# Second DeltaNet half prepared inside the first half's last level

## What is computed

```python
def layer(h, l):
    u = rms_norm(h, attn_norm_w[l])
    (dn_q, dn_k, dn_v, dn_z, dn_b, dn_a, df_q, df_k, df_v, ml_cq, ml_ckv, ml_kr) = split_columns(u @ w_in[l])
    y_dn = gated_deltanet(...)     # two directions, chunked, 4 heads of 128
    y_df = diff_attention(...)     # 4 heads, p0 - lam * p1
    y_ml = mla_attention(...)      # 4 heads, 128 + 64 rotary
    h = h + concatenate([y_dn, y_df, y_ml]) @ w_out[l]
    u = rms_norm(h, ffn_norm_w[l])
    return h + (swiglu(u) if l % 2 == 0 else moe_swiglu(u))   # layer 1: top 2 of 8 experts

def chunk_gated_delta_rule(q, k, v, beta, g):      # per chunk, gc = cumsum(g)
    decay = exp(gc[i] - gc[j]) for i >= j
    a_mat = strict_lower((beta * k) @ k.T * decay)
    value = solve(I + a_mat, beta * v)
    k_cumdecay = solve(I + a_mat, beta * k * exp(gc))
    v_new = value - k_cumdecay @ state
    out = (q * exp(gc)) @ state + ((q @ k.T) * decay) @ v_new
    state = state * exp(g_last) + (k * exp(g_last - gc)).T @ v_new
```

## Time and profile before

| what | us |
|---|---|
| three runs | 1918.44, 1910.54, 1918.0 (median 1918.0) |
| profiled execution, its own time | 1916.52 |
| span of that execution | 1914.7 |
| TensorE busy | 1859.5 (97%) |
| VectorE busy | 1468.5 (77%) |
| ScalarE busy | 1121.1 (59%) |
| GpSimd busy | 101.3 (5%) |
| mixers of layer 0 | from about 136 to 300 |
| mixers of layer 1 | from about 689 to 850 |

### The profile page before, as it was taken

One profiled execution on the slowest core, in us unless ns is written; L12 is line 12 of the kernel. 1 busy time (PEld: TensorE's weight loads), 2 busy tenths in 40 slices (PEclk: granted clock), 3 DMA queues, 4 the chain that ended last, 5 costly groups with the idle time before them and its releaser, 6 DMA issues.

```text
span 1914.7 us, 26250 instructions
## 1 busy us (share of the span) xinstructions
PE 1859.5 (97%) x10606; PEld 1577.0 (82%) x10606; DVE 1468.5 (77%) x1732; ACT 1121.1 (59%) x1241; POOL 101.3 (5%) x95
## 2 busy tenths in 40 slices
PE   9997989999999989989999999999999999999998
PEld 8985768999999967679788888888888888888886
DVE  8759667555459657766888889889888888898986
ACT  5644424433345635344777777777776777777775
POOL 0014030000000022110000000000000000000000
PEclk9999989999999989999999999999999999999999
DMA  7400014454444000034899999999998999999994
GB/s 302 155 29 1 1 34 166 163 172 170 157 177 154 24 28 1 16 118 176 330 353 360 350 350 354 346 350 356 348 362 340 349 351 353 366 352 363 355 363 174
DMA packets 64192, 443.51 MB, mean 232 GB/s; under 512 B 8172, under 2 KB 8204, under 8 KB 13632
## 3 DMA queue, kind: packets, MB, share of 16 engines
q1 hardware_dynamic: 62032, 437.87, 61.6%
q0 software_dynamic: 1760, 3.78, 0.6%
q10 hardware_dynamic: 272, 0.10, 0.0%
HBM read 440.66 MB, written 2.17 MB: 231 GB/s over the span
## 4 chain that ended last, share of the span: by engine, by line
PE 88%; DVE 10%; issue 1%; ACT 1%; DMA 0%; SPq 0%; DVEq 0%; ACTq 0%
PE ps L1951 23%; PE ps L1953 23%; PE ps L1952 23%; PE ps L1964 2%; DVE w_lo L1229 2%; DVE cacc L1321 2%; PE ps L2384 1%; PE ps L2568 1%; PE ps L2370 1%; PE ps L2189 1%; PE ps L2579 1%; PE ps L2389 1%; PE ps L2236 1%; PE ps L2274 1%; PE ps L2273 1%
## 5 line engine op out<-in xcount | busy, mean ns | idle before, releaser
L1286 DVE TENSOR_TENSOR m_lo<-raw,m_hi 128x2048 fp32r<-128x2048 f32 x336 | 768.3, 2289 | 135.9 <-ACT m_hi L864 135.7
L864 ACT ACTIVATE m_hi<-raw 128x2048 fp32r<-128x2048 f32 x336 | 644.1, 1918 | 269.1 <-PE ps L1953 269.1
L1951 PE MATMUL ps<-m_hi,xe_hi 128*128 128x512 f32 x896 | 358.6, 400 | 0.0
L1952 PE MATMUL ps<-m_hi,xe_lo 128*128 128x512 f32 x896 | 353.6, 395 | 0.0
L1953 PE MATMUL ps<-m_lo,xe_hi 128*128 128x512 f32 x896 | 353.6, 395 | 0.0
L1229 DVE TENSOR_TENSOR w_lo<-raw,w_hi 128x1024 fp32r<-128x1024 f32 (+1 forms) x164 | 183.2, 1155 | 105.6 <-ACT w_hi L829 105.6
L1951 PE MATMUL ps<-u_hi,w_hi 128*128 128x272 f32 x800 | 235.1, 294 | 6.5 <-DVE w_lo L1229 4.4
L1953 PE MATMUL ps<-u_lo,w_hi 128*128 128x272 f32 x800 | 231.5, 289 | 0.0
L1952 PE MATMUL ps<-u_hi,w_lo 128*128 128x272 f32 x800 | 230.4, 288 | 0.0
L829 ACT ACTIVATE w_hi<-raw 128x1024 fp32r<-128x1024 f32 (+1 forms) x164 | 159.5, 1002 | 115.0 <-PE ps L1953 106.0
L1953 PEld LDWEIGHTS ps<-m_lo,xe_hi 128*128 128x128 f32 x896 | 168.0, 187 | 41.1
(11 more groups left out here) (404 smaller groups left out, 2610.7 us busy)
## 6 DMA issues: line engine op xcount, KB each, us to landing
raw<-in_moe_units SPq DMA_DIRECT2D x336, 1024.0 KB, 4.9
raw<-in_dense_units SPq DMA_DIRECT2D x57, 1024.0 KB, 5.0
raw<-in_dense_units SPq DMA_DIRECT2D x16, 768.0 KB, 5.6
raw<-in_dense_units SPq DMA_DIRECT2D x8, 896.0 KB, 4.5
w_uq<-in_mla_w_uq SPq DMA_DIRECT2D x2, 768.0 KB, 4.4
mats<-in_c_mats POOLq DMA_DIRECT2D x1, 1216.0 KB, 10.8
h<-in_h_rows SPq DMA_DIRECT2D x2, 544.0 KB, 4.5
bias_rows<-bias_row POOLq DMA_DIRECT2D x1, 1088.0 KB, 25.8
```

The source lines that it names most:

```text
L864: nc.scalar.activation(m_hi[k % RING][:, :], raw[:, slot, :], ACT.Copy).then_inc(m_hi_ready, 1)
L1286: V.tensor_tensor(m_lo[k % RING][:, :], raw[:, mslot(k), :], m_hi[k % RING][:, :].bitcast(F32), ALU.subtract).then_inc(m_lo_ready, 1)
L1951: mm(o, w[0], x[0], start=first, stop=False)
L1952: mm(o, w[1], x[0], start=False, stop=False)
```

## The change

- **Half 0.** Decay, columns and beta of direction 0 follow directly on the last product of queries and keys, in place of five idle products and ahead of the first turn of the others. The column sums are made for both halves at once, eight small products in place of two times four, into a new tile dcol. x of level 0 goes ahead of the rows for the queries.
- **VectorE in half 0.** add, prod, mask, the two small products and TT of level 0 stand ahead of the first probabilities of the differential attention, which were ahead of prod.
- **Identities.** The two copies per half move to ScalarE (begin).
- **Half 1.** It gets its own tiles for the lower triangle, the decay and the query rows (dn_AT1, dn_decay1, dn_QE0 and dn_QE1 of half 1) in the region of the input's split parts, which nobody reads during the mixers. Its decay and beta are made in level 6 of half 0, kb(1, 0) and kb(1, 1) just before TT of level 6 and before r of half 0, low_rows(1) (add, prod, mask) between r and out of half 0. Ten idle products ahead of x(1, 0) go.
- GpSimd's list of instructions and all transfers keep their order.

```diff
                       (("g", o_dn_at), ("b", state_at))] for d in range(2)], [[put(f"dn_r{x}1{d}", [P, H, P]) for x in "gb"] for d in range(2)]
+        dn_at1, dn_decay1, dn_qe10, dn_qe11 = (put(f"dn_{x}1", [P, H, P]) for x in ("AT", "decay", "QE0", "QE1"))
+        dcol = put("dcol", [P, 2, 2, 16])
         put, mark = region(split_at)
...
+                def decay(s):
+                    pe_w("decay", s)
+                    S.mark(nc.scalar.activation(dn_decay[s][:, :, :], heads(ps[:, 3 * s, :]), ACT.Exp), "decay", s)
+
+                def begin(s):
+                    both = bc(ident, 1, 2 * H)
+                    nc.scalar.activation(dn_tt[:, :, :, :].rearrange("p d h n -> p (d h) n"), both, ACT.Copy)
+                    S.mark(nc.scalar.activation(dn_t[:, :, :, :].rearrange("p d h n -> p (d h) n"), both, ACT.Copy), "start", s)
+
...
                     if s == 0:
+                        decay(0)
+                        begin(0)
+                        dve_w("cols")
+                        powers = dcol[:, :, :, 0:12].rearrange("p s d c -> p (s d) c")
+                        S.mark(nc.scalar.activation(powers, powers, ACT.Exp), "expcols")
                         turn_of_others()
                     turn_of_others()
...
                         pe_w("vnew", s, d)
                         S.mark(nc.scalar.activation(batch[d]["X"][:, :, :], heads(ps[:, 2 * d + 1, :]), ACT.Copy), "vnew", s, d)
...
 
+                def key_beta(s, d):
+                    pe_w("beta", s, d)
+                    to = dn_qe[1][1] if d else dn_at[s]
+                    bank = 3 if d else 2
+                    S.mark(V.tensor_tensor(to[:, :, :], kk[:, (s, 1 - s)[d], :, :], heads(ps[:, bank, :]), ALU.mult), "kb", s, d)
+
+                def low_rows(s):
+                    own("kb", s, 1)
+                    link(V.tensor_tensor(dn_at[s][:, :, :], dn_at[s][:, :, :], dn_qe[1][1][:, :, :], ALU.add))
+                    act_w("decay", s)
+                    S.mark(V.tensor_tensor(dn_at[s][:, :, :], dn_at[s][:, :, :], dn_decay[s][:, :, :], ALU.mult), "prod", s)
+                    own("prod", s)
+                    S.mark(V.tensor_tensor(dn_m[0][:, :, :], dn_at[s][:, :, :], bc(mat(M_LV), 1, H), ALU.mult), "mask", s, 0)
+
...
-                    turn_of_others()
-                    pe_w("cols", s)
+                    if s == 0:
+                        pe_w("cols")
+                        sums_of = ps[:, 1, 0:32].rearrange("p (g k c) -> p g k c", k=2, c=4)
+                        col = dcol[:, :, :, :].rearrange("p s d c -> p (s d) c")
+                        link(V.tensor_copy(col[:, :, 0:4], sums_of[:, :, 0, :]))
+                        V.tensor_tensor(col[:, :, 4:8], sums_of[:, :, 1, :], col[:, :, 0:4], ALU.subtract)
+                        S.mark(V.tensor_copy(col[:, :, 8:12], sums_of[:, :, 1, :]), "cols")
+                        key_beta(0, 0)
+                        turn_of_others()
+                        key_beta(0, 1)
+                        turn_of_others()
+                        low_rows(0)
                     for d in range(2):
...
-                        act_w("expcols", s, d)
-                        V.scalar_tensor_tensor(cols[:, c + 12:c + 16], bd[d], -1.0, cols[:, c:c + 4], ALU.mult, ALU.mult)
+                        act_w("expcols")
+                        V.scalar_tensor_tensor(dcol[:, s, d, 12:16], bd[d], -1.0, dcol[:, s, d, 0:4], ALU.mult, ALU.mult)
                     own("mask", s, 0)
+                    act_w("start", s)
                     pair = level_pair(dn_tt, 0)
                     S.mark(V.tensor_tensor(pair, pair, level_of(dn_m[0][:, :, :].rearrange("p h n -> p (h n)"), 0), ALU.subtract), "TT", s, 0)
+                    turn_of_others()
...
+                        if (s, n) == (0, LEVELS - 1):
+                            key_beta(1, 0)
                         if n:
...
                     if s == 0:
                         turn_of_others()
+                        key_beta(1, 1)
                     for d in range(2):
-                        c = 16 * d
...
+                    if s == 0:
+                        low_rows(1)
                     turn_of_others()
...
-                idle_products(5, 0)
+                flat = lambda x: x[:, :, :].rearrange("p h n -> p (h n)")
+
+                def decay(s):
+                    for d in range(2):
+                        i = mm(ps[:, 3 * s, :], mat(M_ST + d), flat(row_parts[s][d][0]), start=(d == 0), stop=(d == 1))
+                    S.mark(i, "decay", s)
+
+                def beta(s, d):
+                    S.mark(mm(ps[:, 2 + d, :], mat(M_ST + d), flat(row_parts[s][d][1]), start=True, stop=True), "beta", s, d)
+
+                dn_pool.wait(pe, l, "rows", 0, 1)
+                decay(0)
+                for g in range(4):
+                    t, d = (g // 2, 1 - g // 2)[g % 2], g % 2
+                    gd = gcol[:, t, 0, 4 * d:4 * d + 4]
+                    mm(ps[:, 1, 8 * g:8 * g + 4], mat(M_TRI + d), gd, start=True, stop=True)
+                    i = mm(ps[:, 1, 8 * g + 4:8 * g + 8], ones, gd, start=True, stop=True)
+                S.mark(i, "cols")
+                beta(0, 0)
...
                         dve_w("qk", 1)
-                    S.mark(mm(ps[:, 3, :], mat(M_ST + 1), flat(row_parts[s][1][1]), start=True, stop=True), "beta", s, 1)
+                        beta(0, 1)
                     turn_of_others()
                     if s == 0:
                         turn_of_others()
-                    for d in range(2):
-                        dve_w("kb", s, d)
-                        S.mark(mm(ps[:, 2 + d, :], ones, flat(row_parts[s][d][0]), start=True, stop=True), "rows", s, d)
                     for n in range(LEVELS):
                         if n == 0:
                             if s:
-                                act_w("decay", s)
-                                idle_products(10, 0)
+                                dve_w("out", 0, 0)
                             dve_w("mask", s, 0)
                         else:
...
                         S.mark(i, "x", s, n)
+                        if n == 0:
+                            for d in range(2):
+                                if s:
+                                    dve_w(("out", "state")[d], 0, 1)
+                                else:
+                                    dve_w("kb", 0, d)
+                                S.mark(mm(ps[:, 2 + d, :], ones, flat(row_parts[s][d][0]), start=True, stop=True), "rows", s, d)
+                            turn_of_others()
+                            if s:
+                                turn_of_others()
+                            else:
+                                meta_first(0)
+                            continue
                         if s == 0 and n < 6:
                             meta_first(n)
+                        if (s, n) == (0, LEVELS - 1):
+                            dn_pool.wait(pe, l, "rows", 1, 1)
+                            decay(1)
+                            beta(1, 0)
                         turn_of_others()
-                        if n == 0:
-                            continue
                         act_w("x", s, n)
                         dve_w("TT", s, n - 1)
...
                         S.mark(i, "up_t", s, n)
+                        if (s, n) == (0, LEVELS - 1):
+                            act_w("decay", 1)
...
```

111 lines of the change are left out of this document (46 added, 65 removed).

## The result

| what | before | after |
|---|---|---|
| median of 11 runs each (us) | 1913.56 (1910.54 to 1918.44) | 1920.7 (1919.32 to 1922.32) |
| ratio to before, of the means | 1 | 1.0032 (95% interval 1.0020 to 1.0044) |
| profiled execution, its own time | 1916.52 | 1919.32 |
| its span | 1914.7 | 1917.2 |

The changed kernel is 0.3% slower: inside the range of the prediction, but on the other side of no change. The runs of before fall into two groups, near 1911.5 and near 1918, and its median moves between them from session to session; the runs of after form one group, above both. So the difference of the two profiles, 2.5, stands for the upper group of before.

What follows compares the result with a forecast made beforehand. TensorE was taken as the bound, with 88% of what ended last. Terms of -1.0, -2.75, 0 and -2.5 sum to -6.25 us, from 1916.52 to 1910.3; 1.5 for the median gives 1911.8, range 1899 to 1924.

Steps and rivals of the forecast that it cites:

- Start, layer 0: Start of half 0 in layer 0: 1.0 us faster, ends -2.8 and +1.0.
- so beta is done at 140.4: Start of half 0, layer 0: TensorE finishes beta at 140.4 instead of 143.2, 2.8 us earlier.
- Together the DeltaNet's own chain is up to 4.2 earlier: Start of half 0, layer 0: 2.8 us from earlier beta plus 1.36 from two copies leaving VectorE.
- The second term: Start of half 0, layer 0: one more probability slowed beside a GpSimd pair, 1.47 instead of 0.50, costs 0.97 us.
- x of level 1 within 1 us: Sign in layer 0: x of level 1 staying within 1 us of its place would confirm that probabilities set the pace.
- Start, layer 1: Start of half 0, layer 1: -1.0 as in layer 0, -1.75 for half the half-clock loss; -2.75 us together.
- Passage, layer 0: Layer 0, passage to half 1: state 4.0 us later, following VectorE chain shorter, net 0; ends -5.5 and +3.3.
- the wait for the rotation: Sign in layer 0's passage: TensorE still waits some us for rotated queries; under 2 us speaks for the faster rival.
- Passage, layer 1: Layer 1, passage to half 1, TensorE the bound: net -2.5 us, ends -3.2 and -0.4.
- The slower one: Both starts: longer first wait for probabilities drops the clock, each start losing 3.5 us; 1925.8 us in all, chance 0.12.
- The faster rival: Passage of layer 0: the 5.49 us wait and the half clock behind it go, -10.7; 1901 us in all, chance 0.20.
- The one in which the change does little: Probabilities pace both starts, layer 0 stays as it is, only layer 1's passage gains; 1915.5 us, chance 0.22.

## Why the prediction was wrong

**Start, layer 0: "I take -1.0", measured +2.4, outside its ends.** The step that failed is "so beta is done at 140.4", and on it "Together the DeltaNet's own chain is up to 4.2 earlier". That is the first beta, and for it the 2.8 held. VectorE needs the second too, which stands behind lambda and two sets of scores, and the second set waited 0.92 for maxima; so the second beta came 1.14 earlier and add 1.84, not 4.2. The DeltaNet work that was put ahead of the probabilities took 3.5 on the timeline, near the 3.8 of the sum, so they came 1.64 later and not 0.4 earlier. The second term was mis-sized too: a set of probabilities beside GpSimd loses up to 2.9, not 0.97. Of the signs named, x of level 1 within 1 us failed: it came 2.5 later, since the probabilities, which do set the pace, came later themselves. Putting back one turn on VectorE takes the whole loss away.

**Start, layer 1: "Together -2.75", measured +0.2 between the two profiles.** The half clock of 693 to 700 went, all 3.3 of it, more than the 1.75 taken; the waits took 3.5. Behind this stands a second error. The baseline was one execution, and that clock fall isn't in each: the second profile of before has none and a start 6.9 shorter. Here a gain read from a stretch at half clock is a gain over some executions only.

**Passage, layer 0: "Net 0", measured -0.07.** The number is luck. Identities and columns alone give -4.3 (61.96 to 57.69), and the early preparation gives it back, 61.89 against 57.66 without it, 1.8 of that through the clock. The sum had the stretch behind the state shorter because VectorE's 3.5 of preparation leave it; but with those 3.5 still there it takes 31.62, and without them 31.95 (35.90 before), while level 6 to the state grew by 3.88 as forecast. Of the signs that the prediction named, the wait for the rotation stayed at 3.3, with another of 3.4 ahead of it.

**Passage, layer 1: "Net -2.5", measured -1.8**, inside its ends: 3.84 added in level 6 and 5.67 gone behind the state, where 4 and 6 were said.

**Rivals.** The slower one had the right place (the first wait for probabilities in both layers) and its condition came true (4.6, past 2.9), but not the mechanism. The clock over the starts is 0.86 and 0.82 where it was 0.90 and 0.77, and TensorE's busy time didn't grow; the wait itself is the loss. With idle products in the waits the clock is 1.00 from 150 to 154, where the changed kernel has 0.50. This agrees with the Trainium skill (TensorE: Matmul & The Clock Gate, section "What's actually happening"), by which activity releases the throttled clock. The faster rival didn't come: in the passage of layer 0 both waits together are 6.7, where one was 5.49. The one in which the change does little left the starts as they are, which they aren't.

**Sum.** Starts +2.4 and +0.2, passages -0.1 and -1.8, in place of -1.0, -2.75, 0 and -2.5: +0.7 where -6.25 stood. A further 2.3 lie in the stretch from x of level 2 to x of level 6 (1.95 and 0.38), which changes from one execution to the next and isn't laid to the change by any run. By whole times the change comes apart in three: columns and identities alone are a gain (0.9971); with the early half 1 added it is gone (0.9997, by intervals that just overlap); with the new start added in its place there is a loss (1.0019); both together have 1.0032. What stays open is how much of the difference of the medians falls of the clock make: each profile is one execution, and no run varied that stretch alone.

## What to carry to other kernels

Before moving a chain up, find the last product that its consumer needs, and ask what that product stands behind on its own queue: the first of two similar products says nothing. What is put ahead of another chain's work on a shared engine costs that chain its full length, and here the other chain set the pace. A stretch at half clock in one profile should be looked for in a second execution before its end is counted as a gain.

## What the runs showed that was not expected

- Two executions of the same program differ by 6.9 us in a stage of some 35 (30.40 and 37.34 in the start of layer 1), from whether the clock falls and whether three VectorE instructions lie beside a GpSimd pair.
- Beside GpSimd a VectorE product of 88x1 took 1.21 where one of 96x1 took 0.15, as long as products of 272 elements: what it loses is set by GpSimd's instruction, not by its own size. This agrees with the Trainium skill (SBUF — State Buffer, section "SBUF: two separate sides"), by which each excludes the other for a whole instruction.
- Idle products brought full clock back in waits of 3 to 5 us in the changed kernel, up to 4.1 a stage. In the kernel with columns and identities alone they gained 2.4 in a passage and, in the starts, 1.5 in layer 1 and nothing in layer 0, where the clock still fell (0.85).
